# Another order of the first layer's start, and VectorE alone on the weight sums of layer 0's down projection

## What is computed

```
h = x                                                    # (264, 1024)
for i in range(2):
    xn = rmsnorm(h, g_attn)
    z = xn @ w_in        # queries, three kinds of keys and values, S5 input u, gates
    A = sparse_attention(z, caches)                      # compressed, selected, window
    y, state = ssm_scan(u, a, log_dt, b, c, d)           # S5 mixer
    h += (sigmoid(gA) * A + sigmoid(gB) * glu(gelu(y))) @ w_o
    gate, value = split(rmsnorm(h, g_ffn) @ w_up)
    h += (gelu(conv(gate)) * value) @ w_down             # w_down is (2816, 1024)
    h += sigmoid(rmsnorm(h, g_ple) @ w_ple_gate) * (p[i] @ w_ple)
```

## Time and profile before

| | us |
|---|---|
| median of 3 runs | 1084.0 (1083.99 to 1086.57) |
| the profiled execution, its own time | 1086.65 |
| its span, first to last instruction | 1085.0 |
| PE busy | 1051.1 (97%) |
| DVE busy | 738.6 (68%) |
| ACT busy | 318.4 (29%) |
| POOL busy | 259.7 (24%) |
| mean granted clock of PE | 0.99 |

### The profile page before, as it was taken

The page is one execution under the profiler, slowest core; times in us unless marked ns, Lnnn a source line. Parts: engine busy times, 40 slices in busy tenths (PEclk is TensorE's granted clock), DMA queues, the critical chain, the costliest instruction groups (busy, mean ns, idle before and its releaser), DMA issues.

```text
span 1085.0 us, 21175 instructions
## 1 busy us (share of the span) xinstructions
PE 1051.1 (97%) x8187; PEld 927.9 (86%) x8187; DVE 738.6 (68%) x1653; ACT 318.4 (29%) x1005; POOL 259.7 (24%) x402
## 2 busy tenths in 40 slices
PE   8899999999999999998999999999999999999996
PEld 5788777778899999998888778777898999999995
DVE  4999805736688878795654876256387788885673
ACT  4535524521221121111335354345112122110021
POOL 4854321002251111342251625010032111120000
PEclk9999999999999999999999999999999999999998
DMA  8745672424585564442536539433354665545441
GB/s 224 229 118 137 170 272 57 118 83 152 155 184 162 167 171 159 146 146 100 178 114 195 153 95 290 147 87 103 117 147 129 176 171 157 155 155 167 137 130 41
DMA packets 218260, 162.54 MB, mean 150 GB/s; under 512 B 25408, under 2 KB 212254, under 8 KB 218080
## 3 DMA queue, kind: packets, MB, share of 16 engines
q1 hardware_dynamic: 208928, 145.72, 45.7%
q0 software_dynamic: 4480, 13.27, 4.3%
q10 hardware_dynamic: 4752, 2.20, 0.8%
HBM read 157.94 MB, written 7.58 MB: 153 GB/s over the span
## 4 chain that ended last, share of the span: by engine, by line
PE 72%; DVE 18%; issue 4%; ACT 3%; SPq 1%; DMA 1%; ACTq 0%; POOL 0%; DVEq 0%; POOLq 0%
PE bank_act L861 28%; PE bank_dve L861 24%; PE bank_dve L1411 9%; PE bank_dve L1188 1%; DVE vpast L2448 1%; DVE vpast L2445 1%; DVE vpast L2446 1%; ACT PT L1560 1%; PE bank_act L1263 1%; DVE PT L2474 1%; PE bank_dve L1004 1%; PE bank_o L1278 1%; DVE kT L2183 1%; DVE z L2506 1%; DVE R L2488 1%
## 5 line engine op out<-in xcount | busy, mean ns | idle before, releaser
L861 PE MATMUL bank_act<-xn,ring 128*128 128x264 f32 x848 | 199.2, 393 | 4.0 <-DVE xn L2140 3.3
L861 PEld LDWEIGHTS bank_act<-xn,ring 128*128 128x128 f32 x848 | 160.9, 193 | 37.8 <-issue 9.5
L861 PE MATMUL bank_dve<-sg,vpast 128*128 128x132 f32 x1056 | 129.6, 278 | 0.3 <-DVE vpast L2448 0.3
L861 PEld LDWEIGHTS bank_dve<-sg,vpast 128*128 128x128 f32 x1056 | 122.5, 190 | 2.4 <-DVE vpast L2448 0.7
L861 PE MATMUL bank_dve<-xn,ring 128*128 128x132 f32 (+1 forms) x704 | 89.6, 281 | 0.0
L861 PEld LDWEIGHTS bank_dve<-xn,ring 128*128 128x128 f32 x704 | 85.2, 190 | 1.2
L861 PE MATMUL bank_dve<-sg,ring 128*128 128x132 f32 (+1 forms) x496 | 71.2, 291 | 0.4 <-DVE sg L2374 0.4
L861 PEld LDWEIGHTS bank_dve<-sg,ring 128*128 128x128 f32 x496 | 64.3, 190 | 2.5 <-DVE sg L2374 0.5
L861 PE MATMUL bank_act<-ring,xn 128*128 128x256 f32 (+1 forms) x256 | 62.2, 397 | 0.0
L861 PEld LDWEIGHTS bank_act<-ring,xn 128*128 128x128 f32 x256 | 48.6, 195 | 9.3 <-issue 0.4
L1560 ACT ACTIVATE PT<-z 128x10 f32<-128x10 f32 x40 | 8.9, 224 | 144.6 <-DVEq L2524 144.6
(11 more groups left out here) (502 smaller groups left out, 2146.1 us busy)
## 6 DMA issues: line engine op xcount, KB each, us to landing
ring<-in_w_up_dram SPq DMA_DIRECT2D x88, 512.0 KB, 5.1
ring<-in_w_in_dram SPq DMA_DIRECT2D x28, 1024.0 KB, 6.2
ring<-in_w_down_dram SPq DMA_DIRECT2D x16, 1024.0 KB, 5.0
ring<-in_w_glu_dram SPq DMA_DIRECT2D x16, 512.0 KB, 4.5
ring<-in_w_o_dram SPq DMA_DIRECT2D x8, 1024.0 KB, 5.1
ring<-in_w_ple_gate_dram SPq DMA_DIRECT2D x8, 1024.0 KB, 5.1
ring<-in_w_down_dram SPq DMA_DIRECT2D x8, 768.0 KB, 4.4
PT<-in_cache_cmp_dram SPq DMA_DIRECT2D x64, 64.0 KB, 2.7
```

The costliest lines, as they stand in the source:

```text
L861: ins = pe.matmul(out, lhsT, rhs, start=(k == 0), stop=(k == nk - 1))
```

## The change

It has two independent parts.

In the start of layer 0: PE multiplies fewer zeros (once 448 and once 256 columns instead of six times 448). `params_turned(0)` moves from behind job 0 into the prologue, between the first and the second half of x's tiles; DVE's `prep_steps` and `prep_params` move with it, between its copies of tiles 3 and 5 (`prep_params` leaves out the first eight columns, which are there already). PE's wait for the early tables moves from before job 0 to after it, in front of `sum_squares(0)`; DVE's moves from before `add_squares` to after `norm(0)`. `add_squares` and `prep_angles` now follow the last copy directly. ACT issues the two loads of window keys after the copies of jobs 0 and 1 instead of before the roots. The parameter job counts among the prologue's jobs.

In the down projection of layer 0: `SHARED_FROM` is 12, so POOL makes no weight sums there, and DVE makes all four of every chunk. This is what it already does in layer 1.

```diff
-SHARED_FROM = 3
+SHARED_FROM = 12
@@
-ACT_PRO, DVE_PRO = 4, 5
+ACT_PRO, DVE_PRO = 4, 6
@@ dve_stages
-        ("params", own), ("norm0", 1), ("c", 2 * own), ("k0", own), ("h0", own),
+        ("norm0", 1), ("c", 2 * own), ("k0", own), ("h0", own),
@@ params_taken
-    return dve_jobs(0, "params", 1) if L == 0 else dve_jobs(L - 1, "down", 3 + 1)
+    return 4 if L == 0 else dve_jobs(L - 1, "down", 3 + 1)
@@ PE, prologue
-                    for _ in range(n):
-                        pe.matmul(bankO[:, 0:448], qpad[:, 0:P], qpad[:, P:P + 448], start=True, stop=True)
+                    pe.matmul(bankO[:, 0:n], qpad[:, 0:P], qpad[:, P:P + n], start=True, stop=True)
 
                 pe.wait_ge(zeroed, 1)
-                zeros(2)
+                zeros(448)
                 pe.wait_ge(ident_in, 32)
                 pe.wait_ge(g_in, 16)
                 pe.transpose(dve_bank()[:, 0:KD], prm_rows[0:KD, :], ident[0:KD, 0:KD]).then_inc(dve_ready, 1)
-                zeros(1)
+                zeros(256)
                 pe.wait_ge(x_in, 32)
                 for k in range(KD):
                     if k == 2:
-                        zeros(1)
                         pe.wait_ge(x1_in, 16)
                     if k == KD // 2:
-                        zeros(2)
+                        params_turned(0, dve_bank)
                         pe.wait_ge(x2_in, 16)
@@ PE, layer
                     if jobs == SUM_AT[L]:
                         if L == 0:
-                            params_turned(0, dve_bank)
+                            pe.wait_ge(early_in, 16 * EARLY)
                         sum_squares(0)
@@ PE
             assert run(0, prologue, None, None)[0:2] == (ACT_PRO, DVE_PRO)
-            pe.wait_ge(early_in, 16 * EARLY)
@@ ACT
-                for s in range(2):
-                    window_keys(s)
+                if L > 0:
+                    for s in range(2):
+                        window_keys(s)
                 std(L, 0)
@@ ACT, the jobs
+                    if L == 0 and jobs < 2:
+                        window_keys(jobs)
@@ DVE
-                dve.tensor_copy(prm2[:, L, :], take(base)[:, 0:32 + 3 * ST]).then_inc(dve_freed, 1)
+                first = KD if L == 0 else 0
+                dve.tensor_copy(prm2[:, L, first:], take(base)[:, first:32 + 3 * ST]).then_inc(dve_freed, 1)
@@ DVE
             for k in range(1, KD, 2):
+                if k == 5:
+                    prep_steps(0)
+                    prep_params(0, 0)
                 bank = take(0)
@@ DVE
-            prep_steps(0)
+            for k in range(KD):
+                add_squares(0, 0, k)
+            prep_angles(0)
             dve.sem_inc(h_done, KD)
-            dve.wait_ge(early_in, 16 * EARLY)
@@ DVE
+                norm(0)
                 if L == 0:
-                    for k in range(KD):
-                        add_squares(0, 0, k)
-                    prep_params(0, base)
-                    prep_angles(0)
-                norm(0)
+                    dve.wait_ge(early_in, 16 * EARLY)
```

## The result

The changed kernel took 1076.98 us in the median, the kernel before 1084.35 beside it: a ratio of 0.9928, 95% interval 0.9914 to 0.9942, so 7.4 us faster; forecast were 1074.6 us and 9.4.

A forecast was written before the change was run, and what follows sets the result against it. Bound by PE's waits: a chain of loads, ACT and DVE in the first 53 us, then DVE in layer 0's down projection. 3.55 + 4.3 + 1.6 = 9.45 off the 1084.0 median gives 1074.6 us, range 1071 to 1079.5.

The forecast's parts named there:

- Part one: Layer 0's start reordered: the drive matmuls begin at 49.3 instead of 52.83, 3.55 us earlier.
- the sentence on the zero matmuls: Layer 0's start: zero matmuls taken out ahead of job 0 only filled waiting for x, so worth nothing by themselves.
- Rival 3: Layer 0's start: clock low in job 0, 3.3 us lost, part one near 0.3, time 1077.8; chance 0.08.
- the 11.1: Layer 0's start: time in us taken for the parameters' arrival, letting DVE copy them; bounds 10.6 and 13.76.
- The first clock loss: First drive matmuls after PE's 1.78 us gap: 16 took 5.41 us instead of 3.72, a 1.69 loss taken as staying.
- rival 1: Both clock losses, at the drive and in the down projection, go: 1.7 us more, 1072.9; chance 0.21.
- Part two: Layer 0's down projection, all sums on DVE: 4.3 us of PE waits and 1.6 of clock loss go.
- Waits of 4.3: Layer 0's down projection: PE's waits for DVE shrink by 0.4 + 1.14 + 1.47 + 1.3 us; 0.8 stays.
- The second clock loss: Layer 0's down projection, after PE's 2.10 us wait: 16 matmuls took 3.52 us, some 1.6 more; taken as gone.
- The lengthening that was taken at 12.7: Layer 0's down projection: DVE operations run 12.7 us longer beside POOL's nine pairs, against at most 11.7 for 18 sums.
- the marks that the prediction named: Trace signs of right or wrong: parameter copy, x's last tile, job 0, PE gap, drive, down-stage DVE operations and waits.
- Rival 5: Layer 0's down projection: 18 sums simply added, POOL's hold no cause; DVE 7.8 us late, 1088.3; chance 0.03.

The follow-up runs named there:

- e1: The changed kernel run again with no edit, against the kernel before: 1076.94 us, ratio 0.9925.
- e4: The changed kernel with the six zero matmuls of 448 columns put back in their places: 1073.41 us, ratio 0.9897.
- e2: The changed kernel with POOL making its share of layer 0's down sums again (start part alone): 1086.5 us, ratio 1.0017.
- e7: The changed kernel with the six zero matmuls of 448 columns back and POOL's shared sums as before: 1082.51 us, ratio 0.9988.
- e6: The kernel before with only the zero matmuls cut as in the change: 1085.46 us, ratio 1.0009.
- e8: e4 with the window-key issue put back ahead of the roots on ACT: 1073.79 us, ratio 0.9908.
- e9: The changed kernel with two zero matmuls of 448 columns put back, only at PE's wait for the parameters: 1074.66 us, ratio 0.9908.
- e11: e4 a second time: 1074.98 us, ratio 0.9900.
- e12: e3 a second time: 1076.43 us, ratio 0.9917.
- e10: e3 with the window-key issue alone moved behind jobs 0 and 1: 1074.61 us, ratio 0.9906.
- e3: The kernel before with DVE making all of layer 0's down-projection sums (down part alone): 1075.71 us, ratio 0.9922.
- e5: e3 plus 18 POOL additions between two buffers nobody else touches, at the places of its former sums: 1088.49 us, ratio 1.0037.

## Why the prediction was right or wrong

**Part one failed in the sentence on the zero matmuls.** They "cost and give nothing by themselves", it says, and the sum has them at nothing, with the clock left to a rival: e1 to e4 (3.5 us) and e2 to e7 (4.0) say otherwise. Rival 3, given 0.08, is what happened: a slow job 0, at 5.96 us from 15.18 to 21.14 instead of 3.72, and on top of it four tiles of x at 0.82 instead of 0.52, 3.4 together. Its price of 3.3 came out, though it had job 0 alone at 7.4 and the tiles at full speed; its chance was too low: the row for it, PE standing 3 us for the parameters behind hardly any work, was named in the rival's own sentence. The record of the granted clock in the traces says the same: it begins at 19.78 us in e1, 19.73 in e2 and 18.70 in e6, the three with few zero matmuls and an unfilled wait, and at 4.7 to 10.6 in the ten others. Of the two rules of the Trainium skill weighed there, the one of "TensorE: Matmul & The Clock Gate", Part 1 (throttled is the default, activity releases it), is the one that came out, and the runs agree with it.

The other, of the Trainium skill's "DMA: Bandwidth & Descriptors", "Anatomy of one DMA", is told there of loads that GpSimd issues, while these are issued on ACT's queue; by the prediction's estimate from it the parameters come at 12.5. In the seven executions with the new place of the parameters (e1, e2, e4, e7, e8, e9, e11) DVE's copy of the steps starts at 10.5 to 11.3, 0.5 to 0.6 us behind the last packet of that queue, and PE turns the parameters at 11.0 to 11.6, in e11 at 12.04. So the 11.1 was good, though the reading behind it stopped short: in the profile of before the queue's last packet comes at 10.8, not at 10.5 to 10.6.

**The base was one draw.** 3.55 us were subtracted from the median, but worked out against an execution 2.65 us above it, whose key issue was the longest of five. The drive in the start order of before lay at 52.83, 50.75, 50.88 and 53.40 us (the last, e12, with the clock at 0.59 from 27 to 31 us); with the parameters early and a warm PE at 49.27, 49.19, 49.23, 48.73 and, with the clock lost, 50.84. The means differ by 2.5 us. And less than that arrives. From 120 us to the down projection the executions differ by their clock losses: there is one between 115 and 126 us in e1, e2, e4, e9, e10 and e11 (the 0.68 above) and in none of the others, and one between 160 and 176 us in all but e2 and e8. The way takes 314.2 to 314.8 us with both, 313.3 to 313.5 with the second alone, 313.8 with the first alone (e2, where it lasts longer) and 311.8 with neither (e8). Busy times from 115 to 126 us of e2_start_only, then of e8_keys_first:

```profile
115.00:126.00 11.00, 8.42 (x30) 6.21 (x29) 9.98 (x25) 5.47 (x16) 5.06 (x10) 0.69 0.76 214
```

```profile
115.00:126.00 11.00, 9.88 (x52) 8.46 (x53) 10.79 (x27) 4.52 (x14) 5.01 (x10) 1.00 0.96 253
```

The first of these losses does not follow from an early drive alone: e7 and e8, with the drive at 49.2, do not have it, and e1, at 51.70, does. Nor does PE wait longer there when the drive is early: it stands 1.7 to 2.6 us for the key rows in all thirteen. What decides is open. What was left is 1.5 to 2.3 us (e7 against before, e4 against e3, e11 against e12); in each of these pairs the intervals overlap or touch, and all three point the same way.

**The first clock loss** was taken as staying and went, but its 1.69 us were never worth that: the way from the drive to 120 us is 68.44 with it in before, 67.93 and 67.85 without it in e3 and e12 (e5, with it, has 68.57, and e6, without, 67.97). Some 0.5 us; rival 1 was priced three times too high. Part of the rest is waited for: without the loss PE stands 0.7 us for DVE at later drive matmuls (e3, e6, e12), with it not at all (before, e5).

**Part two was right in its mechanism and too small.** Waits of 4.3 were to go and 0.8 to stay: PE's idle time in the stage fell from 5.37 to 0.96, with 0.9 at the wait foreseen. The second clock loss, 1.6, went in every kernel without POOL's sums or additions (5.20 us at 0.67 are 1.7). The lengthening that was taken at 12.7 is some 14 (14.0 in e5; in before, the 58.41 of e1 less 10.8 for the 18 sums leaves 47.6, and DVE is busy 61.69). Together 6.1 of the 7.08 us; the last 1.0 is in PE's busy time, partly in the blocks behind a wait (2.04 us for 1.96). Beyond the stage, layer 1 from its heads on is 1.1 us shorter wherever POOL makes no shared sums (271.6 against 272.7, once the clock losses between 685 and 710 us, some 1.7 us in before, e2, e5, e6 and e8, are taken off). It lies in layer 1's up projection: 0.4 spread over blocks 180 to 197 us behind the heads, and two steps of 0.4 beside waits such as this one, in PE's timeline of before, which e1_whole and e5 do not have:

```profile
911.18 2.97 PE L861 MATMUL bank_dve<-sg,vpast 128*128 128x132 f32 x24 [0.15 <-DVE vpast L2448]
```

Why it is there was not tried and stays open. 7.1 and 1.1 are 8.2; the runs of e3 and e12 gained 8.0 and 8.4.

Of the marks that the prediction named, the parameters on DVE near 12 (11.86), no gap between job 2 and the columns, no DVE operation of one product over 1 us and one PE wait under 1 came true; x's last tile near 14.2 (it ended at 15.1) and the drive at 49 to 50 did not, and "job 0 over 4.5 us", named as the mark of its being wrong, was there.

**Rival 5**, the sums simply added because POOL's hold was no cause, fell: DVE with 18 sums more was busy 3.3 us less, and e5 shows the hold by itself.

**The sum.** Part two 8.0 to 8.4 instead of 5.9, part one a loss of 1.2 (e3 to e1, where the intervals overlap) to 1.8 (e2 by its ratio) instead of a gain of 3.55. Two errors of opposite sign left the forecast 2.4 us low: that the time fell within the range was luck as far as part one goes. The better kernels are e4 (and e11, the same kernel), e8, e9 and e10, at 1073.4 to 1075.0 us: the sums on DVE, and either the keys behind the first jobs or the parameters early with the wait filled. Between these four the runs do not decide.

## What to carry to other kernels

Before filler work is cut from a start, look at what the engine's clock does behind the wait that it fills: two matmuls of zeros there (e9 against e1, 2.3 us) were worth as much as the whole reordering. Do not subtract from a median a gain that was read off one long execution; a queue issue or a clock loss that varies from run to run is only partly in the median. Where GpSimd is given work to relieve VectorE, add up how much longer VectorE's own operations get beside it: here 18 additions taken over, 10.8 us of its time, cost it some 14.

## What the runs showed of the hardware

- The clock column does not show a clock that has not yet risen: e1_whole reads 1.00 from 10 to 21 us, where x's tiles took 1.6 times and the first half of job 0 1.9 times as long as in e4. The clock record in that trace begins at 19.78 us, with the rise. A clock that falls after having risen shows (0.66 in e11, 15 to 20 us). At a start, durations have to be read.
- Waits of the same length are followed by a clock loss or not: 1.78 and 1.76 us ahead of the drive by 16 matmuls in 5.41 us (before, e5), 1.75, 1.76 and 1.60 by 3.72 (e3, e6, e12).
- The issue of one load on ACT's queue took between 0.81 and 3.63 us at the same place of the program, and 0.38 to 0.65 us a few us later, behind job 1. What sets it is open.
- Two DVE sums of 128x512 that lie beside GpSimd additions of 1.4 to 1.6 us took 1.5 us each instead of 0.69, though the two engines share no data (e5).
